# 192 gathered rows instead of 176, the half-filled block of tokens packed for the output products, and longer runs in two DMA streams of a retrieval block

## The reference

```
n2 = rms_norm(h, g_norm2) * (1 + scale2) + shift2
h  = h + gate2 * peer(n2)
out = rms_norm(h, g_final)

peer, for each token t: 8 heads, each picks 16 of 128*128 = 16384 experts (product keys,
  two top-16 of 128, then top-16 of their sums), softmax weights g over the 16:
    out[t] = sum over the 128 picked experts k of  gelu(n2[t] . U[k]) * g[t,k] * V[k]
```

## Time and profile before

| | |
|---|---|
| median of 3 runs | 1623.19 us |
| span of the profiled execution | 1618.1 us, 5.1 us below the median of the runs |
| PE busy | 1570.4 us, 97% |
| DVE busy | 1403.7 us, 87% |
| ACT busy | 641.8 us, 40% |
| POOL busy | 624.0 us, 39% |
| mean granted TensorE clock | 0.988 |
| moved by DMA | 436.11 MB, mean 270 GB/s |

### The profile page before, as it was taken

One profiled execution on the slowest core, in us unless ns is written; L12 is line 12 of the kernel. 1 busy time (PEld: TensorE's weight loads), 2 busy tenths in 40 slices (PEclk: granted clock), 3 DMA queues, 4 the chain that ended last, 5 costly groups with the idle time before them and its releaser, 6 DMA issues.

```text
span 1618.1 us, 23763 instructions
## 1 busy us (share of the span) xinstructions
PE 1570.4 (97%) x7899; PEld 1291.7 (80%) x7899; DVE 1403.7 (87%) x2781; ACT 641.8 (40%) x955; POOL 624.0 (39%) x531
## 2 busy tenths in 40 slices
PE   6999999999999999999999999999999999999997
PEld 3777764665557899988888888898888888888886
DVE  6888877764999999979888998989999998989886
ACT  4234654241122666663333333333333333333233
POOL 0000000010555500016655666656555676767520
PEclk8999999989999999999999999999999999999998
DMA  8432215542212355589999999999999999999981
GB/s 349 167 150 79 79 52 197 221 155 78 92 72 73 106 205 199 209 307 402 402 380 386 375 380 389 394 392 387 355 396 358 387 362 398 347 380 355 403 301 64
DMA packets 127851, 436.11 MB, mean 270 GB/s; under 512 B 12832, under 2 KB 35360, under 8 KB 122016
## 3 DMA queue, kind: packets, MB, share of 16 engines
q1 hardware_dynamic: 74112, 247.92, 41.2%
q0 software_dynamic: 52224, 184.62, 29.6%
q10 hardware_dynamic: 1440, 2.62, 0.4%
HBM read 407.29 MB, written 27.79 MB: 269 GB/s over the span
## 4 chain that ended last, share of the span: by engine, by line
PE 71%; DVE 19%; DMA 4%; issue 3%; ACT 2%; POOL 0%; DVEq 0%; SPq 0%; ACTq 0%; POOLq 0%
PE ps L970 23%; PE ps L900 23%; PE ps L671 10%; PE ps L662 6%; PE ps L958 3%; DMA graw<-gmat 3%; PE ps L827 3%; DVE low L1886 2%; DVE Vs L1874 1%; DVE Us L1857 1%; DVE big L1886 1%; DVE att L1713 1%; DVE att L1724 1%; DVE big L1711 1%; DVE big L1729 1%
## 5 line engine op out<-in xcount | busy, mean ns | idle before, releaser
L970 PE MATMUL ps<-Vs,As 128*128 128x512 f32 x2286 | 535.6, 390 | 2.5 <-DVE As L1877 2.5
L970 PEld LDWEIGHTS ps<-Vs,As 128*128 128x128 f32 x2286 | 425.9, 188 | 86.1 <-DVE Vs L1874 1.6
L900 PE MATMUL ps<-xs,Us 128*128 128x336 f32 x2832 | 461.2, 318 | 5.1 <-DVE Us L1857 4.2
L900 PEld LDWEIGHTS ps<-xs,Us 128*128 128x128 f32 x2832 | 441.4, 188 | 22.6 <-issue 10.0
L594 POOL DMA_INDIRECT big<-pv,islot x176 | 255.9, 1454 | 144.6 <-DVE low L1916 50.9
L1338 ACT ACTIVATE big<-ps 128x352 f32<-128x352 f32 x96 | 44.7, 465 | 340.4 <-PE ps L900 281.2
L1874 DVE TENSOR_TENSOR Vs<-big,Vs 128x1024 fp32r<-128x1024 f32 x127 | 155.2, 1222 | 17.1 <-ACT Vs L1344 14.3
L662 PE MATMUL ps<-big 128*128 128x512 f32 (+1 forms) x416 | 160.3, 544 | 1.3 <-ACT big L1040 1.3
L1916 DVE SCALAR_TENSOR_TENSOR low<-big,low 128x1024 f32<-128x1024 f32 x128 | 157.0, 1280 | 0.0
L1344 ACT ACTIVATE Vs<-big 128x1024 fp32r<-128x1024 f32 x127 | 134.0, 1055 | 42.9 <-PE ps L970 40.7
L594 POOL DMA_INDIRECT low<-pu,islot x88 | 119.7, 1360 | 72.5 <-DVE colv L1886 53.9
(11 more groups left out here) (249 smaller groups left out, 2087.2 us busy)
## 6 DMA issues: line engine op xcount, KB each, us to landing
big<-puT SPq DMA_DIRECT2D x128, 512.0 KB, 3.5
big<-pv SPq DMA_DIRECT2D x64, 1024.0 KB
big<-stream SPq DMA_DIRECT2D x31, 1024.0 KB, 5.2
gmat<-big SPq DMA_DIRECT2D x11, 2048.0 KB, 7.3
graw<-gmat SPq DMA_DIRECT2D x30, 512.0 KB
low<-wada SPq DMA_DIRECT2D x28, 512.0 KB, 4.8
work<-wada SPq DMA_DIRECT2D x14, 512.0 KB, 5.6
graw<-gmat SPq DMA_DIRECT2D x15, 384.0 KB
```

Source lines behind the costliest of these rows:

```text
L900: mm = nc.tensor.matmul(ps[:, 6 + e, DEAD:ET], a, xs[:, b, k, :], start=(k == 0 and a is hi and b == 0), stop=(k == KT - 1 and a is lo))
L970: mm = nc.tensor.matmul(ps[:, 2 * b + half, :], a, v_parts[:, w, half * T:(half + 1) * T], start=(opens and a is hi and w == 0), stop=(las ...
```

## The change

- NEXT = 4: 64 tokens of groups of 16 go the row way, so NROWS = 192, and the dense way has 320 columns; the first 64 of the 384 token places are empty. UB goes from 60 to 62, VE from 122 to 124. BUILT is 80 and FILLED 10.
- The first token block of the output products has 64 live tokens. Hi and lo of the activations are written alternately (`a_part`, a step of two floats), so that one 128-column load holds both parts of the 64 tokens. The block takes 4 products and not 6; its third product (lo x lo) comes along. The sum of the hi and lo places is made once, at the end, with a matrix `fold`.
- The groups' gathering products go to banks 6 and 7, at block 126 instead of 114. The token blocks are finished in the order 0, 2, 1, 3.
- V comes from a host-arranged copy `pvP` with 8 KB runs. `gmat` is laid out by groups of eight expert blocks: stores in 1 KB runs, reads in 4, 4 and 2 KB runs.
- GpSimd's fetches are unrolled, without the copy to `islot`.
- A fourth pass of the transposition that repeats a group's tokens (at gap block 8, its copy at 9), no products that clear dead columns, no zero fill of the piece (L1281).

```diff
-NEXT = 3
+NEXT = 4
-UB = 60
-VE = 122
+UB = 62
+VE = 124
+HALF = P - XB
+ORDER = (0, 2, 1, 3)
...
-        As = sb("As", [P, 2, 2, DT], f32r)
+        As = sb("As", [P, 2, 2 * ET], f32r)
+        def a_part(A, w):
+            return A.rearrange("p (t w) -> p w t", w=2)[:, w, :]
...
-                    sp.dma_start(gmat[k:k + 1, :, :].rearrange("a p f -> (a p) f"),
-                                 piece[:, k % PRING, :, :].rearrange("p i t -> p (i t)")
+                    sp.dma_start(gmat[:, :, k - FIRST, :].rearrange("q p f -> p q f"),
+                                 piece[:, pslot(k), :, :].rearrange("p (q a) t -> p q (a t)", a=GRUN)
...
-                             pv[bass.ds((g * BODY + 2 * e) * P, 2 * P), :].rearrange("(a p) f -> p a f", p=P)
+                             pvP[bass.ds(g * (BODY // 2) + e, 1), :, :].rearrange("a p f -> (a p) f")
...
-                             gmat[FIRST:PIECES, :, bass.ds((g * BODY + q * GRUN) * HT, GRUN * HT)][h].rearrange("h p f -> p h f")
+                             gmat[bass.ds(g * (BODY // GRUN) + q, 1), :, h, :].rearrange("a p h f -> (a p) (h f)")
...
+            def fetch(r):
+                if r >= ROWBUF:
+                    pool.wait_ge(row_used, r - ROWBUF + 1)
...
+            for r in range(2 * NROWS):
+                fetch(r)
...
-                        mm = nc.tensor.matmul(ps[:, 6 + e, DEAD:ET], a, xs[:, b, k, :],
+                        mm = nc.tensor.matmul(ps[:, 6 + e, 0:ET], a, xs[:, b, k, :],
...
             def output_block(o, b, a_parts, v_parts, last=False, opens=False):
-                hi, lo = (a_parts[:, w, b * P:(b + 1) * P] for w in range(2))
-                for a, w in ((hi, 0), (hi, 1), (lo, 0)):
+                if b == 0:
+                    both = a_parts[:, 0:P]
+                    pairs = ((both, 0), (both, 1))
+                else:
+                    hi, lo = (a_part(a_parts, w)[:, HALF + (b - 1) * P:HALF + b * P] for w in range(2))
+                    pairs = ((hi, 0), (hi, 1), (lo, 0))
...
+            def fold_halves(src, part, begins=False, ends=False):
+                for half in range(2):
+                    mm = nc.tensor.matmul(ps[:, 6 + half, :], part, src[:, half * T:(half + 1) * T],
+                                          start=begins, stop=ends)
...
+                    if b == 1:
+                        pe.wait_ge(unfolded_ready, 1)
+                        fold_halves(unfolded, fold, ends=True).then_inc(folded, 1)
...
-                v.tensor_tensor(A[:, 1, XB:DT], act_t, A[:, 0, XB:DT].bitcast(f32), ALU.subtract).then_inc(alo_ready, 1)
+                v.tensor_tensor(a_part(A, 1), act_t, a_part(A, 0).bitcast(f32), ALU.subtract).then_inc(alo_ready, 1)
```

More of the change, by code:

```diff
@@ L502, in load_turn @@
                     if first and e == 2:
[L503 to L504 removed]
+                        all_stored(sp)
                     if not (first and e < 2):
@@ L998, in dense_turn @@
                         hidden(g * LATE + (EARLY + i), i % 2)
-                    if last and d == 2:
+                    if last and d == BODY - 2:
+                        pe.wait_ge(gel_ready, XT + 2)
                         pe.wait_ge(row_used, NROWS + XTOK)
                         for q in range(NEXT):
-                            for half in range(2):
-                                nc.tensor.matmul(ps[:, half, :], gath[q], acc_ext[q][:, half * T:(half + 1) * T],
-                                                 start=False, stop=False)
+                            fold_halves(acc_ext[q], gath[q], begins=(q == 0))
                     if last and d >= BODY - 2:
@@ L1254, in _ @@
                   ).then_inc(spread_ready, 1)
+            for q in range(NEXT - 1):
+                repeat_ext(q)
             def gelu_early(n):
@@ L1362, in _ @@
             dense_turn(TURNS - 1, True)
-            for b in range(TB):
-                deviation(b)
+            act.wait_ge(row_used, 2 * NROWS)
+            act.wait_ge(v_done, XT + 1)
+            f(unfolded, ps[:, 0:2, :].rearrange("p h d -> p (h d)"), ACT.Copy).then_inc(unfolded_ready, 1)
+            for i, b in enumerate(ORDER):
+                deviation(i, b)
         @block.vector
@@ L1902, in row_weights @@
                 step(v.tensor_tensor(act_w[:, :], act_w[:, :], dots[:, :], ALU.mult))
+                settled()
+                pairs = ident[:, :].rearrange("p (t w) -> p w t", w=2)
+                step(v.tensor_tensor(fold[:, XB:P], pairs[:, 0, :], pairs[:, 1, :], ALU.add))
+                step(v.memset(fold[:, 0:XB], 0.0))
                 settled()
@@ L1953, in _ @@
                         step(v.tensor_tensor(acc[:, 0, :], acc[:, 0, :], acc[:, 1, :], ALU.add))
-                        dve.wait_ge(h_here, 16 * (TB + 2))
-            residual(0)
-            residual(1)
+                        dve.wait_ge(h_here, 16 * (TB + 1))
+            residual(ORDER[0])
+            residual(ORDER[1])
             norm(0)
-            for b in range(2, TB):
-                residual(b)
-                norm(b - 1)
+            for i in range(2, TB):
+                residual(ORDER[i])
+                norm(i - 1)
             norm(TB - 1)
```

177 lines of the change are left out of this document (85 added, 92 removed).

## The result

The changed kernel takes 1611.22 us (median of 4 runs, 1609.42 to 1614.24), the kernel before 1622.78 (4 runs, 1622.03 to 1624.70). The ratio is 0.9944, with a 95% interval of 0.9927 to 0.9961: 0.56% less time, where 1.37% was forecast. The direction held; the gain is 11.6 us where 22 were expected.

A forecast was written before the change was run, and what follows sets the result against it. TensorE paced the kernel at 6.86 us a block, VectorE and DMA 8% and 3% behind. Building, start, dots, adds and end summed to 1591.7, plus 4 for uneven patterns: span 1596, plus 5.1 to the median: 1601 us, range 1573 to 1633.

The forecast's parts named there:

- Building and T0: Stage up to block 0's weights' product: 714.39 - 6.5 (four fewer steps) + 0.6 - 0.8 (zero fill) = 707.7.
- The start of the dense stage: Blocks 0 to 2: 12.6 us as before plus 2.2 for the last store, block 2 at 722.5.
- the 2.2 us for the last store: Start of the dense stage: last piece's store in 2048 runs of 1 KB, 2.2 us more (0 to 5) than 7.90.
- Dots: Blocks 2 to 62: DMA paces, 165.6 MB at 409 GB/s, 405 us, 6.75 a block, above VectorE's 6.45.
- Row weights and groups' adds: After block 62: row weights 5 us on VectorE's path, then 64 group rows in 20.7 blocks of 7.10, 147 us.
- Late adds: Up to block 124: 41.3 blocks at DMA's 6.62 (2.71 MB at 409 GB/s), 273.4 us; VectorE at 6.50.
- The end: Output of block 123 to last scaling: 18.0 + 6.9 (gatherings) + 15.6 = 40.5 us, 36.8 before; + 3.1 to span's end.
- The 4 us allowed for uneven patterns: Whole span: engines' patterns uneven between blocks with and without hidden, 0.03 us a block added, 4 us.
- VectorE alone: Dots and late adds: longer runs lift queues to 425 GB/s or more, VectorE alone paces; 1580 us, chance 0.18.
- DMA slower than before: Dots and late adds: added rows cost more than is saved if queues hold under 396 GB/s; 1636 at 389, chance 0.16.
- The step of two floats: Activations written two floats apart: 0.22 us on each of 126 blocks, about 15 us; 1616, at the double 1631, chance 0.09.
- TensorE no faster: TensorE's products with interleaved loads run no faster, 6.86 a block stays the pace; 1623 us, chance 0.04.

The follow-up runs named there:

- e7_u_first: Changed kernel with the U load for block 2 ahead of the last store of the weights' matrix, V's second load behind it: 1608.32 us, 0.9932.
- e5_old_runs: Changed kernel with both old layouts: V in 4 KB runs, the weights' matrix stored in 16 KB and read in 1 KB runs: 1620.98 us, 0.9996.
- e15_old_gmat: Changed kernel with only the weights' matrix in its old layout (16 KB stores, 1 KB reads), V in 8 KB runs: 1611.24 us, 0.9952.
- e1: Changed kernel with each dot reading 512 of its 1024 columns, gathers as they were: 1609.58 us, 0.9927; dots 406.7 us.
- e2: Changed kernel with the second of each two V blocks not loaded, engines' work as it was: 1592.54 us, 0.9813; dots 396.3 us.
- e8_tail: Changed kernel with token blocks 2 and 3 finished before the packed block, gatherings and fold (order 0, 2, 3, 1): 1610.51 us, 0.9942.
- e3_18_products: Changed kernel with the packed block's second product made twice, so an output has 18 products again: 1624.02 us, 1.0017.
- e11_loop: Changed kernel with GpSimd's fetches back in the loop of 16 with copies to islot: 1614.18 us, 0.9960.
- e4: Changed kernel with the 64 group adds going round the four accumulators instead of one group after the other: 1606.08 us, 0.9907.

## Why the prediction was right in sign and short in size

The mechanism held in the middle: DMA is the bound of the dots. The size did not, 0.56% for 1.37%. The steps that failed are sizes of terms, above all the start of the dense stage, the late adds and the end. The forecast gave 1595.7 for the span; the profiled one was 1607.5, 11.8 more. By its own steps:

**Building and T0** (707.7 forecast, 710.6 measured, +2.9). A step takes 1.62 us as said; VectorE waits 6.8 us for ScalarE in this stage, 5.7 before, and the stage's first step came 1.6 later. So the +0.6 for the fourth pass and the lists was too small; which of the two took the time isn't separated.

**The start of the dense stage** (14.8 forecast, 19.0 measured, +4.2). The step that failed is the 2.2 us for the last store alone. The store took 10.7 us to its landing for 7.9 before, 2.8 more, near what was priced. But the U behind it came later still: ScalarE's wait for it grew from 4.36 to 8.59 us. TensorE's idle time then cost a second time, since that hidden, at the low clock, took 6.15 us for 3.68. `e7_u_first`, with U ahead of the store, takes 11.6 us for the same blocks: the stall needs the store ahead of U. But that order was there before the change. Why the wait grew is only in part known. It isn't the store's short runs alone: with the old layout of the store (`e5_old_runs`, `e15_old_gmat`) the wait is still 7.65 and 7.69 us and the start 18.3 and 18.2, while the kernel before with the new layout has 7.45 and 18.2. One thing that differs is V's first loads, which stand ahead of the store in the same queue: they were issued 4.9 us before it in the kernel before, and 3.1 in the changed one. No run moved them alone.

**Dots** (405 forecast, 407.5 measured, +2.5). Right in mechanism and nearly in size: DMA decides (`e1`, `e2`), at 405 GB/s in the mean, where 409 was taken. The part that was missed is that VectorE, at 6.45 by its sum, runs at 6.61 when no landing holds it (`e2`); so the distance between the two was 0.18 us a block and not 0.30. TensorE was short too: an output of 16 products takes 3.73 us to the next start (1575.94 to 1579.67) and not 3.63, with 3.52 for a hidden 6.37 a block and not 6.29. The Trainium skill ("DMA: Bandwidth & Descriptors", "Where 436 GB/s comes from") gives 435 GB/s for the fabric and about 358 for HBM on a core. The traces agree with the first (414 at most in a slice of 40 us) and again not with the second, since this kernel held 405 over 390 us.

**Row weights and groups' adds.** VectorE paces, and alternating moved it. To block 83 the forecast's terms give 5 + 147 + 0.3 x 6.62 = 154.0 us; 150.4 were measured, 3.6 less. Every add was priced at 1.39, but only an add that follows another one of its group takes that.

**Late adds.** The step that failed is 6.62 a block: 41 blocks make 271.4 us, and 277.5 were measured (6.77), 6.1 more. Nothing here shows DMA's 6.62 by itself, since with V halved the blocks still take 6.68: VectorE, at 6.50 by its sum, is again slower than its sum and as long as DMA's term. Both stages together: +2.4, the smaller because one error hid part of the other.

**The end** (38.8 forecast from block 124, 42.6 measured, +3.8). The step that failed is what stands behind the gatherings. They themselves cost a little less than was priced (6.5 us to the next product at 1586.14, for 6.9), and the work ahead of them 18.8 for 18.0. Behind them the forecast had 15.6 us, with two residuals and two scalings after the fold. In the trace 18.3 us pass from 1586.14 to the last scaling's end: VectorE waits 7.87 us for PSUM, and three of the four token blocks' residuals and all four scalings come after that, 13.1 us. The token block that is to be its first out of PSUM needs the same 20 products as the folded one (1591.39), so hardly any of this work went beside TensorE's. `e8_tail` gets 2.9 back.

The 4 us allowed for uneven patterns were not seen as a term of their own; they are in the sums above. So 2.9 + 4.2 + 2.5 + 2.4 + 3.8 - 4 = 11.8. Around the span lay 2.2 us and not 5.1 (-2.9), and the median lies 1.5 above the profiled execution. DMA as the bound of the dots did not fall. What fell are sizes, most of them to the same side, and it is luck that the sum is not further off: the groups' adds came in 3.6 us under and the time around the span 2.9 under, which hid 6.5 us.

**The rivals.** VectorE alone (1580): out by `e1`. DMA slower than before (1636): out, since the queues held 405 and not 389; but the margin was thin: `e5_old_runs`, at 5 to 7 GB/s less in the two long stages, has nothing left of the gain. The step of two floats: out (its price in the forecast, about 15 us on VectorE, doesn't come from its own terms: 0.22 in 21 blocks and 0.12 in 41 make 10). In the changed kernel the product that reads activations and writes them, and its successor:

```profile
847.00 0.49 DVE L1902 TENSOR_TENSOR As<-big,As 128x320 fp32r<-128x320 f32 x1
847.40 1.22 DVE L1911 CUSTOM_DVE_ANT_0 low<-low,big 128x1024 f32<-128x1024 f32 x1
```

They start 0.40 us apart, where 0.41 was worked out for 320 contiguous elements. The Trainium skill ("SBUF — State Buffer", the note on 16-byte cachelines) says that two hits in a line keep full speed, and this row agrees. TensorE no faster (1623): out, with outputs of 3.89 us busy for 4.24 and `e3_18_products` as its counterpart.

## What to carry to other kernels

When the engine that paces is made faster, sum the work of the next two for a block before anything else: here the second stood 3% behind, so an 8% faster TensorE was worth 3% in the dots. Once the queues are full, a saving of bytes for a block counts and an overtaking in the queue may only make another load late; spreading the same bytes over two more blocks in each part, with the adds alternating, gave more than the whole change had (1596.21 us against 1615.07 and 1619.74 for the kernel before, timed together). Small terms at the two ends of a stage (a store ahead of a load, a gathering ahead of the first residual) took 9.8 of the 21.3 us that the long stages brought, so price the order and not only the work.

## What the runs showed of the hardware

**TensorE's clock after a gap.** Three hiddens that followed idle times of 4.81, 3.55 and 5.04 us took 6.15 to 6.35 us, and the granted clock of their windows fell. One of them, and then two of the windows:

```profile
845.68 6.17 PE L911 MATMUL ps<-xs,Us 128*128 128x320 f32 x24 [3.55 <-DVE Us L1881]
```

```profile
720.00:730.00 10.00, 7.16 (x30) 6.95 (x31) 3.59 (x5) 3.73 (x6) 7.87 (x8) 0.66 0.90 313
840.00:850.00 10.00, 6.45 (x26) 5.77 (x25) 8.06 (x13) 1.43 (x2) 3.90 (x4) 0.71 1.02 409
```

6.17 against 3.68 us is the lower of the two levels (1.2 and 2.4 GHz) over most of the 24 products, and a granted clock of 0.66 and 0.71 is a window that stood at that level for more than half of its 10 us. Three more (at 1116.78, 1287.65, 1502.35) took 5.31 to 5.33 us after gaps of 1.98 to 2.36, while one after 2.58 (at 1009.32) and seven after 0.94 to 1.47 took 3.78, so the gap alone doesn't decide. The six together cost TensorE 12.5 us; the kernel before has no such hidden in the whole stage. An engine that is no longer the bound is thus not as fast in its work as it was when it was full.

**Spread.** Executions of the changed kernel differ more than those of the kernel before: 1609.26 to 1618.60 in 11 runs and 1605.04 to 1617.91 in 10 of `e11_loop`, against 1616.88 to 1622.95 in 23 of the kernel before in the same batch. That DMA as the bound is the reason is likely but not shown. The stages that move are those in which DMA is full: in the profiles of five kernels that do the same there (the changed one twice, `e4`, `e8`, `e11`) the dots take 407.4 to 414.0 us and the late adds (blocks 83 to 124) 276.7 to 286.3. The others hardly move: the groups' adds take 149.9 to 150.4 in the four of these that don't alternate them, and the end 42.6 with the old order. So a gain below 5 us can't be read from a few runs, nor from the dots or late adds of one profile; from a stage whose length repeats it can.
